# Setup merged into the in-projection's stage, and bias tiles read back from shifted copies in DRAM

## The reference, cut to what matters

```
xn = rmsnorm(x, norm_mix[0])            # over the 1024 features
p  = xn @ nsa_w_in                      # q (1024), k/v of three branches (1536), gates (48)
...
bias[t, s, head] = rel_bias[rel_bucket(qpos[t] - kpos[s]), head]      # added to the scores
logits = where(dist >= 0, q @ k + bias, -1e30)
```

## Time and profile before

| | |
|---|---|
| median of 3 runs | 2560.46 us |
| the profiled execution | 2560.77 us |
| its span | 2559.1 us |
| mean granted TensorE clock | 0.963 of full speed |
| busy: DVE, ACT, POOL | 1060.6, 577.2, 1039.7 us |
| HBM read, written | 170.80 MB, 28.81 MB |
| DMA packets | 49947, 193.74 MB, mean 76 GB/s |

### The profile page before, as it was taken

The page is one execution under the profiler, slowest core; times in us unless marked ns, Lnnn a source line. Parts: engine busy times, 40 slices in busy tenths (PEclk is TensorE's granted clock), DMA queues, the critical chain, the costliest instruction groups (busy, mean ns, idle before and its releaser), DMA issues. The chain is left out here.

```text
span 2559.1 us, 38344 instructions
## 1 busy us (share of the span) xinstructions
PE 2338.8 (91%) x15282; PEld 1754.0 (69%) x15282; DVE 1060.6 (41%) x1957; ACT 577.2 (23%) x1328; POOL 1039.7 (41%) x912
## 2 busy tenths in 40 slices
PE   6999799789999999999996999999998989999997
PEld 4776444456777777667775778677785767777775
DVE  2001777344430242367886545363543044302412
ACT  1001566321000000135553323232420010000000
POOL 1331345245654464465653131121215456534640
PEclk9999899799999999999998999999998999999998
DMA  6632100451211221211125020110202212112110
GB/s 242 211 106 89 33 1 1 160 191 66 82 62 71 83 82 66 112 66 50 66 70 54 6 100 6 48 54 21 84 6 103 90 64 78 66 66 99 66 66 38
DMA packets 49947, 193.74 MB, mean 76 GB/s; under 512 B 15650, under 2 KB 24610, under 8 KB 33522
## 3 DMA queue, kind: packets, MB, share of 16 engines
q1 hardware_dynamic: 45922, 175.76, 20.1%
q0 software_dynamic: 3856, 15.61, 2.0%
HBM read 170.80 MB, written 28.81 MB: 78 GB/s over the span
## 5 line engine op out<-in xcount | busy, mean ns | idle before, releaser
L1498 PE MATMUL ps<-hid,ring 128*128 128x288 f32 x768 | 194.8, 410 | 23.1 <-DVE hid L1594 23.1
L1498 PE MATMUL ps<-xn,ring 128*128 128x288 f32 x768 | 201.9, 412 | 8.9 <-DVE xn L1578 8.4
L1498 PEld LDWEIGHTS ps<-hid,ring 128*128 128x128 f32 x768 | 146.4, 191 | 64.8 <-DVE hid L1594 24.9
L1498 PEld LDWEIGHTS ps<-xn,ring 128*128 128x128 f32 x768 | 146.5, 192 | 53.4 <-issue 8.0
L1524 ACT ACTIVATE p<-ps 128x288 f32<-128x288 f32 x48 | 19.7, 411 | 631.5 <-PE ps L1498 631.5
L218 PE MATMUL ps<-xn,ring 128*128 128x288 f32 x640 | 157.7, 410 | 2.8 <-ACTq L562 2.8
L1562 POOL TENSOR_TENSOR prod<-prod,rstd 128x1152 f32<-128x1152 f32 x32 | 83.8, 2620 | 179.9 <-DVE prod L1640 163.3
L218 PEld LDWEIGHTS ps<-xn,ring 128*128 128x128 f32 x640 | 122.9, 192 | 37.2 <-ACTq L562 2.9
L2747 PE MATMUL ps<-xn,ring 128*128 128x288 f32 x512 | 138.3, 416 | 3.6 <-PE ps L2812 3.6
L1498 PE MATMUL ps<-x_sum,wsum 128*128 128x288 f32 x512 | 134.1, 416 | 3.2 <-DVE x_sum L1581 2.5
L744 POOL TENSOR_SCALAR ring<-ring,fac 128x128 f32<-128x128 f32 (+2 forms) x96 | 92.2, 976 | 103.2 <-DVE fac L976 103.2
(11 more groups left out here) (449 smaller groups left out, 4806.8 us busy)
## 6 DMA issues: line engine op xcount, KB each, us to landing
ring<-in_w_mlp SPq DMA_DIRECT2D x64, 1024.0 KB, 4.9
ring<-in_w_gdn_in SPq DMA_DIRECT2D x16, 1024.0 KB, 4.9
ring<-in_w_nsa_in SPq DMA_DIRECT2D x10, 1024.0 KB, 8.3
ring<-in_w_gdn_z SPq DMA_DIRECT2D x8, 1024.0 KB, 4.9
x<-in_seq_state SPq DMA_DIRECT2D x4, 2048.0 KB, 8.6
out_seq_state<-x SPq DMA_DIRECT2D x4, 2048.0 KB, 11.2
ring<-in_w_gdn_out SPq DMA_DIRECT2D x8, 1024.0 KB, 5.7
out_win_old<-in_win_rows POOLq DMA_DIRECT2D x1, 8064.0 KB, 47.4
```

Source lines behind the costliest of these rows:

```text
L1498: mm = nc.tensor.matmul(S.ps[:, base + BANK[p], 0:HT], stationary(p, blk.units[pair // 4], pair % 4), moving(blk.kind, p, pair), start=pai ...
```

## The change

The block `setup_stage` is gone; its work is the first part of `nsa_in_stage`, and its tiles lie beside that stage's. x is loaded in eight chunks with a semaphore each, the even ones on SP's queue, the odd ones on ScalarE's. The four weight slots are issued right behind x, ahead of line_sel and the table. The norm comes first on TensorE and the line behind it; VectorE copies the line in the middle of the norm (`between`). The in-projection waits for scaled chunks one by one. In place of the flip products SP stores `line` 128 times per head (near) and 8 times per head (rows), each row in full, and reads it back with a row step one less than the pitch, which lands the tiles in their final order. The copy of the old window waits for the first product.

```diff
-def norm_scalar(act, S, n):
+def norm_scalar(act, S, n, arrived=None):
     for k in range(KD):
+        if arrived is not None:
+            act.wait_ge(arrived[k], 16)
         S.nc.scalar.activation(S.xn[:, k], S.x[:, k], ACT.Square).then_inc(n.squared, 1)
...
-def norm_vector(dve, S, n):
+def norm_vector(dve, S, n, between=None):
...
+    if between is not None:
+        between()
     dve.wait_ge(n.root, 1)
...
+def setup_loads(sp, S, u):
+    for k in range(0, KD, 2):
+        sp.dma_start(S.x[:, k], S.dram["x"][:, k]).then_inc(u.x_in[k], 16)
+    sp.dma_start(S.normw[:], S.dram["normw"]).then_inc(u.norm_in, 16)
+    dense_prefetch(sp, S, S.dense["nsa_in"])
+    sp.dma_start(u.line_sel[:], S.dram["line_sel"]).then_inc(u.line_in, 16)
+    sp.wait_ge(u.table_set, 1)
+    sp.dma_start(u.table[0:BUCKETS, :], S.dram["rel_bias"]).then_inc(u.line_in, 16)
+    sp.dma_start(S.pages[:], S.dram["pages"]).then_inc(S.pages_in, 16)
+    sp.dma_start(S.cst[:], S.dram["cst"]).then_inc(u.const_in, 16)
+    sp.dma_start(S.gatew[:], S.dram["gate_w"]).then_inc(u.const_in, 16)
+
+def setup_bias(sp, S, u):
+    sp.wait_ge(u.line_sb, 2)
+    near, rows = S.near_dram[0:1, :], S.rows_dram[0:1, :]
+    sp.dma_start(bass.AP(near.tensor, 0, [[128 * NEAR, H], [NEAR, 128], [1, NEAR]]),
+                 u.line[:, DMAX - 255:DMAX - 255 + NEAR].unsqueeze(1).broadcast_to([H, 128, NEAR])).then_inc(u.line_out, 16)
+    sp.dma_start(bass.AP(rows.tensor, 0, [[TD * ROW, H], [ROW + 1, TD], [1, PAST + 2 * TD - 1]]),
+                 u.line[:, 0:PAST + 2 * TD - 1].unsqueeze(1).broadcast_to([H, TD, PAST + 2 * TD - 1])).then_inc(u.line_out, 16)
+    sp.wait_ge(u.line_out, 32)
+    sp.dma_start(S.toep[:], bass.AP(near.tensor, 127, [[NEAR - 1, 128], [128 * NEAR, H], [1, 256]])).then_inc(u.bias_in, 16)
+    sp.dma_start(S.rowb[:], bass.AP(rows.tensor, TD - 1, [[ROW, 128], [1, PAST + TD]])).then_inc(u.bias_in, 16)
+
+def setup_scalar(act, S, u):
+    for k in range(1, KD, 2):
+        act.dma_start(S.x[:, k], S.dram["x"][:, k]).then_inc(u.x_in[k], 16)
+    norm_scalar(act, S, u.norm, u.x_in)
+
+def setup_tensor(pe, S, u):
+    pe.wait_ge(u.ones_set, 1)
+    norm_tensor(pe, S, u.norm)
+    pe.wait_ge(u.line_in, 32)
+    pe.wait_ge(u.table_set, 1)
+    nc.tensor.matmul(S.ps[0:16, 2, :], u.table[:], u.line_sel[:, 0:512], start=True, stop=True)
+    nc.tensor.matmul(S.ps[0:16, 3, 0:LREV - 512], u.table[:], u.line_sel[:, 512:LREV], start=True,
+                     stop=True).then_inc(u.line_mm, 1)
+    pe.wait_ge(u.line_sb, 2)
+
+def setup_vector(dve, S, u):
+    dve.wait_ge(u.norm_in, 16)
+    def lines():
+        dve.wait_ge(u.line_mm, 1)
+        v.tensor_copy(u.line[:, 0:512], S.ps[0:16, 2, :]).then_inc(u.line_sb, 1)
+        v.tensor_copy(u.line[:, 512:LREV], S.ps[0:16, 3, 0:LREV - 512]).then_inc(u.line_sb, 1)
+    norm_vector(dve, S, u.norm, lines)
...
         def _(sp):
+            setup_loads(sp, S, setup)
+            for k in range(KD):
+                sp.wait_ge(setup.x_in[k], 16)
             sp.dma_start(S.x_dram[:], raw[1]).then_inc(x_out, 16)
             sp.dma_start(pages(0)[:, PP], S.dram["cmp_pe"][:, 0]).then_inc(pe_in, 16)
             sp.dma_start(pages(2)[:, PP], S.dram["cmp_pe"][:, 1]).then_inc(pe_in, 16)
+            setup_bias(sp, S, setup)
             dense_loads(sp, S, d)
...
+            sp.wait_ge(setup.const_in, 32)
+            sp.wait_ge(setup.bias_in, 32)
...
         def _(pool):
-
+            setup_gpsimd(pool, S, setup)
+            pool.wait_ge(d.product, 1)
             pool.dma_start(S.out["win_old"], S.dram["win_rows"][:, TD:, :]).then_inc(copied, 16)
             pool.wait_ge(S.pages_in, 16)
             for u in (0, 2, 1):
                 if u == 1:
                     pool.wait_ge(x_out, 16)
+                    pool.wait_ge(setup.norm.scaled, KD)
...
-            dense_products(pe, S, d, lambda k: S.xn[:, k])
+            setup_tensor(pe, S, setup)
+            dense_products(pe, S, d, lambda k: S.xn[:, k], setup.norm.scaled)
             def gates():
+                pe.wait_ge(setup.const_in, 32)
...
-        S.line_dram = nc.dram_tensor("line_scratch", [H, LREV], F32)
+        S.near_dram = nc.dram_tensor("near_scratch", [H * 128, NEAR], F32)
+        S.rows_dram = nc.dram_tensor("rows_scratch", [H * TD, ROW + 1], F32)
```

More of the change, by code:

```diff
@@ L41 @@
 DMAX = PAST + TD - 1
+NEAR = 383
+ROW = 540
 def constants():
@@ L49, in constants @@
     c["ident"] = (i == j)
-    c["flip"] = (i + j == 127)
-    c["flip8"] = (i // 8 == j // 8) & (i % 8 + j % 8 == 7)
     c["incl"] = (i <= j)
@@ L305, in norm_vector @@
                                in1=S.rstd[:, 1], op0=ALU.mult, op1=ALU.mult).then_inc(n.scaled, 1)
-def setup_stage(S):
-    nc = S.nc
[L311 to L398, removed]
@@ new lines, with __init__ @@
+class Setup:
+    def __init__(self, S, sb):
+        self.table, self.line = sb("table", [64, 16]), sb("line", [16, LREV])
+        self.line_sel = sb("line_sel", [64, LREV])
+        self.ones_set, self.table_set, self.table_zero = S.sem("ones_set"), S.sem("table_set"), S.sem("table_zero")
+        self.x_in = [S.sem(f"x{k}_in") for k in range(KD)]
+        self.norm_in, self.line_in, self.const_in = S.sem("norm_in"), S.sem("line_in"), S.sem("const_in")
+        self.line_mm, self.line_sb = S.sem("line_mm"), S.sem("line_sb")
+        self.line_out, self.bias_in = S.sem("line_out"), S.sem("bias_in")
+        S.pages_in = S.sem("pages_in")
+        self.norm = Norm(S, "norm0", 0)
@@ new lines, in setup_scalar, with setup_gpsimd @@
+def setup_scalar(act, S, u):
+    for k in range(1, KD, 2):
+        act.dma_start(S.x[:, k], S.dram["x"][:, k]).then_inc(u.x_in[k], 16)
+    norm_scalar(act, S, u.norm, u.x_in)
+def setup_gpsimd(pool, S, u):
+    g = S.nc.gpsimd
+    g.memset(S.ones[:], 1.0).then_inc(u.ones_set, 1)
+    g.memset(S.eps[:], EPS).then_inc(u.ones_set, 1)
+    g.memset(u.table[:], 0.0).then_inc(u.table_zero, 1)
+    pool.wait_ge(u.table_zero, 1)
+    g.memset(u.table[BUCKETS:BUCKETS + 1, :], NEG).then_inc(u.table_set, 1)
@@ new lines, in setup_tensor @@
+def setup_tensor(pe, S, u):
+    nc = S.nc
+    pe.wait_ge(u.ones_set, 1)
[7 more added lines that the diff above has]
+def setup_vector(dve, S, u):
+    v = S.nc.vector
+    dve.wait_ge(u.norm_in, 16)
[4 more added lines that the diff above has]
+    norm_vector(dve, S, u.norm, lines)
@@ L432, in nsa_in_stage @@
         gate_t = sb("cmp_gate_t", [3 * H, T])
+        setup = Setup(S, sb)
         w1 = S.ring[:, 2:4].rearrange("p s (o i c) -> p s o i c", o=2, i=HALF)
@@ L561, in _ @@
             a_ = nc.scalar
+            setup_scalar(act, S, setup)
             act.sem_inc(d.bank_free, 4)
@@ L602, in _ @@
             v = nc.vector
+            setup_vector(dve, S, setup)
             def prompt(u):
@@ L3140, in build @@
             S.npool = dram["cache_cmp"].shape[1]
-            setup_stage(S)
             S.qkv = sbn("qkv", [128, 20, T])
```

## The result

The changed kernel takes 2573.3 us (median of 8 runs, 2570.8 to 2576.7) where the kernel before takes 2562.5 beside it (8 runs, 2558.8 to 2569.5): ratio 1.0040, 95% interval 1.0027 to 1.0053. It is slower by 10.7 us, and outside the predicted range (to 2571). The profiled execution took 2572.58 us.

What follows compares the result with a forecast made beforehand. TensorE's serial chain, started by the setup, was taken to bound the kernel: 2560.77 - 16.1 (earlier start) + 13.6 (late refill) + 2.1 (clock) = 2560.4 us; likeliest case 2555 to 2566, 8 in 10 within 2546 to 2571.

Steps and rivals of the forecast that it cites:

- The start: Setup: the first in-projection matmul starts at 29.7 us instead of 45.85, set by the copied line; 16.1 us earlier.
- The stores' rate: In-projection: the near and rows stores from 16 partitions run at 115 GB/s, done at 59 us if undisturbed.
- Rival A: In-projection: the stores run at the toep_rev load's 348 GB/s, a 1 to 4 us wait, 2546 to 2550 us; chance 0.30.
- Who traps what: In-projection: the old window's copy holds back the stores' last packets until 83 to 87; stores done at 95.8 us.
- The step that failed: Behind the stores' end at 95.8: start 1.1, reads 6.8, refill 2.6, landing 1.3 us.
- refill 4: In-projection: the first weight refill queued on SP behind the stores' wait and the reads, in at 107.6 us.
- rival B: In-projection: piled-up GpSimd page copies slow SP's stores, reads and refill; a 25.7 us wait, 2572.5 us; chance 0.17.
- Group 4: In-projection: the matmuls that need refill 4, beginning 256 records in, at 94.0 us.
- the stall: In-projection: TensorE stands ahead of Group 4 until refill 4 is in, 13.6 us.
- The clock: In-projection, behind the stall: TensorE falls to 1.2 GHz again, costing 2.1 us.
- A TensorE chain that moves as one piece with its start: Behind the setup: almost everything shifts with its start if nothing new interrupts; TensorE busy 2338.8 of 2559.1 us.

Runs made afterwards that it cites:

- late window: The changed kernel with the old window's copy moved out of the stage, issued by GpSimd at the start of the prompt attention: 2549.95 us, ratio 0.9958.
- after: The changed kernel itself, against the kernel before: 2573.3 us, ratio 1.0040.

## Why the prediction was wrong

- **The start was right**: 28.93 forecast as 29.7, 16.9 us earlier instead of 16.1, by the forecast way: VectorE waits for the line's product, which waits for the table behind the weights. The line was copied by 24.3 (25.1).
- **The stores' rate was near**: 103 GB/s but for the first 0.3 MB, taken as 115; half of the stores' counts were in at 61.1 (59 for all, undisturbed). Rival A fell: it gave under 15 us to landing, and the first half of the counts alone took 36.8.
- **Who traps what was right, in other amounts.** I had the copy's data begin at 42 to 46, with 43% of the stores unfinished and 43 packets on each of 8 engines behind it, 0.53 MB. In fact they began 14 us behind the issue, at 52, not 6.4; all but about 15 rows an engine got through before or beside the copy, and the copy ended at 95.4 instead of 83 to 87. The two errors cancel, which is luck: stores done 95.6, forecast 95.8.
- **The step that failed** is the one behind it: "Then SP issues the reads, which start 1.1 us later: ... refill 4 at 107.6", 11.8 us from the stores' end to the refill's landing (its 1.1 and 1.3 us stand in no row). It was 18.7 us (95.7 to 114.4). I had the refill issued at once behind two reads; SP was held for 6.97 us at the second. Undisturbed (late window) the same steps took 13.4 us: 3.1 until the refill was issued (60.61 to 63.71) and 10.3 to landing, 1.6 above my sum. Of the other 5.3, 4.5 stand ahead of the refill's issue (7.6 instead of 3.1), the rest behind it. Beside the reads GpSimd's page copies moved 0.94 MB between 96 and 104 us, against 0.36 MB from 60 to 68 with the late window. That is rival B's mechanism; that it is the cause is argued from these counts, since no run took the page copies away. B's price for this step, 98.5 to 119.7, was 21.2 us: the measured 18.7 lies between it and my 11.8. Group 4 was also wanted 1.2 us sooner (92.8, forecast 94.0). So the stall is 21.6, not 13.6.
- **The clock** cost 1.0 us behind the stall (what is left of the stage's time), forecast 2.1. So the stage ends with -16.9 + 21.6 + 1.0 = +5.7, where my sum had -0.4.
- **What the sum didn't have** is the 5.9 us behind the stage. "A TensorE chain that moves as one piece with its start" failed: the same work behind the start of attention took 2300 to 2310 us in the profiled executions. The granted clock went with it; its trigger wasn't isolated. The sum put this at nothing, and the range, built from terms of this stage alone, was too narrow: with the stall as measured and nothing behind the stage, the time would have been 2560.77 + 5.7 = 2566.5, inside it.

## What to carry to other kernels

Before a wait for DMAs is put in front of a refill loop, list what every queue starts in that time: on the engines that carry it, a long copy on another queue lets the waited-for transfer through at one packet per turn, and the refills inherit that wait. Moving the copy, or the dependent DMAs to the copy's own queue ahead of it, was worth 21 to 24 us here; making the stores 2.5 times as fast was worth 13, because the reads behind them were trapped instead. Two DMAs that count up one semaphore have no landing of their own in the profile; go by the sizes of their packets. For the range, look first how far the runs of the unchanged kernel spread and whether the clock goes with it: here 8 us below the median and 10 above it.

## What the runs showed of the hardware

- A store that repeats 16 partitions to DRAM ran at 103 GB/s with all 16 DMA engines 91% busy in the records; from 128 partitions the same 1532-byte rows ran at 257 GB/s. Its first microsecond ran at 338 GB/s from the 16 partitions too.
- An issue can hold its engine when the queue is behind: a 128-row read held SP for 2.5 us on a quiet queue, 7.0 in after and 25.3 and 44.2 when the old window's copy ran beside it, always behind a DMA of 2048 rows.
- GpSimd's copy moved its first data 14 us after its issue while the slow stores filled SP's queue, and 6.4 us in the kernel before. With the fast store, and the copy issued at 40.41, GpSimd's queue had moved 0.52 MB by 44 us, and the copy was in after 43.7 us instead of 56.6. So the delay goes with what SP's queue is doing; how isn't shown.
- Where both queues have work on an engine, they are served packet for packet: 479 to 480 in 10 us with packets of 4 KB against 1 KB, 24 to 24 in 8 us with packets of 64 KB against single rows of the stores. The Trainium skill (DMA: Bandwidth & Descriptors, "Queues, rings and completion order") says that an engine takes turns between queues at packet granularity: the counts agree.
